# A router's hand-over between two expert paths: 48 instead of 32 tokens leave the feature matmuls, and 32 instead of 16 gathered rows come during the sums

## What is computed

```
q = (xt @ w_q).reshape(T, PEER_HEADS, 2, half)
s1, s2 = q0 . keys1, q1 . keys2              # 128 scores each, per head
v1, i1 = lax.top_k(s1, 16);  v2, i2 = lax.top_k(s2, 16)
sc, pos = lax.top_k(v1 + v2 (all 256 pairs), 16);  gate = softmax(sc)
u = jnp.take(u_tab, eb, axis=0)              # 128 rows of 1024 per token
a = jnp.einsum('nhkd,nd->nhk', u, xb)
w = jax.nn.gelu(a) * gb
vv = jnp.take(v_tab, eb, axis=0)
y = jnp.einsum('nhk,nhkd->nd', w, vv)
x = layer_norm(alpha * x + y)
```

## Time and profile before

| | |
|---|---|
| median of three runs | 1434.01 us (1432.75 to 1435.45) |
| the profiled execution | 1433.48 us, its span 1431.8 us |
| granted TensorE clock, mean over the span | 0.997 |
| busy in the span: PE, DVE, ACT, POOL | 1406.7, 1087.3, 606.7, 903.4 us |
| moved by DMA | 415.41 MB, mean 290 GB/s |

### The profile page before, as it was taken

How to read it: one execution, slowest core, us unless ns; L and a number is a source line. 1 busy time by engine, 2 the same in 40 slices (tenths; PEclk the granted TensorE clock), 3 DMA queues, 4 the chain that set the end, 5 groups by cost and what they waited for, 6 DMA issues and landing times.

```text
span 1431.8 us, 24761 instructions
## 1 busy us (share of the span) xinstructions
PE 1406.7 (98%) x8045; PEld 1248.2 (87%) x8045; DVE 1087.3 (76%) x2324; ACT 606.7 (42%) x1019; POOL 903.4 (63%) x595
## 2 busy tenths in 40 slices
PE   9999999999999999999999999999999999999996
PEld 5888878888999999999999999878888888888885
DVE  5366666688999998858774885987777777777786
ACT  5666751324333354454544443333333333333332
POOL 3422331335599978979888786766666666666744
PEclk9999999999999999999999999999999999999998
DMA  6213120423689979999999899999999999999981
GB/s 243 75 50 113 59 90 1 147 84 102 197 316 342 323 259 395 417 389 418 418 417 399 341 381 407 383 388 387 371 374 374 372 366 360 367 368 366 372 315 59
DMA packets 138959, 415.41 MB, mean 290 GB/s; under 512 B 13904, under 2 KB 56656, under 8 KB 136720
## 3 DMA queue, kind: packets, MB, share of 16 engines
q1 hardware_dynamic: 80128, 240.69, 45.9%
q0 software_dynamic: 42064, 151.15, 26.8%
q10 hardware_dynamic: 16704, 22.81, 4.3%
HBM read 363.89 MB, written 50.14 MB: 289 GB/s over the span
## 4 chain that ended last, share of the span: by engine, by line
PE 76%; DVE 8%; DMA 5%; POOL 4%; issue 3%; ACT 2%; SPq 1%; DVEq 0%; ACTq 0%; POOLq 0%
PE banks L2019 12%; PE banks L2021 11%; PE banks L2020 11%; PE banks L1964 11%; PE banks L1965 11%; PE banks L1966 11%; DMA raw<-v_tab 3%; POOL lo L501 2%; PE banks L2081 2%; PE banks L2237 1%; PE banks L2238 1%; POOL rows L822 1%; PE banks L2174 1%; DMA rows<-u_rows,expert_at 1%; DVE rows L1454 1%
## 5 line engine op out<-in xcount | busy, mean ns | idle before, releaser
L501 POOL TENSOR_TENSOR lo<-raw,hi 128x1024 fp32r<-128x1024 f32 x224 | 540.2, 2413 | 416.5 <-ACT hi L495 396.5
L1964 PE MATMUL banks<-x1T_hi,hi 128*128 128x352 f32 (+3 forms) x1168 | 389.9, 334 | 1.3 <-ACT kept L1106 1.0
L1965 PE MATMUL banks<-x1T_lo,hi 128*128 128x352 f32 (+3 forms) x1168 | 384.6, 329 | 0.0
L1966 PE MATMUL banks<-x1T_hi,lo 128*128 128x352 f32 (+3 forms) x1168 | 383.6, 328 | 0.0
L495 ACT ACTIVATE hi<-raw 128x1024 fp32r<-128x1024 f32 x291 | 305.6, 1050 | 57.0 <-DMA raw<-u_t 37.4
L2019 PE MATMUL banks<-hi,wgt_hi 128*128 128x512 f32 x750 | 292.1, 389 | 2.0 <-DVE wgt_lo L1811 1.9
L2020 PE MATMUL banks<-lo,wgt_hi 128*128 128x512 f32 x750 | 291.8, 389 | 0.0
L2021 PE MATMUL banks<-hi,wgt_lo 128*128 128x512 f32 x750 | 291.8, 389 | 0.0
L1964 PEld LDWEIGHTS banks<-x1T_hi,hi 128*128 128x128 f32 x1168 | 219.8, 188 | 6.2 <-ACT kept L1106 1.3
L1966 PEld LDWEIGHTS banks<-x1T_hi,lo 128*128 128x128 f32 x1168 | 220.3, 189 | 4.4
L1965 PEld LDWEIGHTS banks<-x1T_lo,hi 128*128 128x128 f32 x1168 | 220.1, 188 | 3.9
(11 more groups left out here) (245 smaller groups left out, 1846.7 us busy)
## 6 DMA issues: line engine op xcount, KB each, us to landing
raw<-u_t SPq DMA_DIRECT2D x128, 512.0 KB
raw<-v_tab SPq DMA_DIRECT2D x128, 512.0 KB
g_scratch<-stage SPq DMA_DIRECT2D x12, 2048.0 KB
gelu_scratch<-gelu ACTq DMA_DIRECT2D x116, 192.0 KB
ga<-gelu_scratch SPq DMA_DIRECT2D x29, 768.0 KB
gg<-g_scratch SPq DMA_DIRECT2D x14, 1536.0 KB
raw<-w SPq DMA_DIRECT2D x26, 512.0 KB
raw<-w_pq SPq DMA_DIRECT2D x16, 512.0 KB
```

The lines of the kernel that those rows point to most:

```text
L501: eng.tensor_tensor(l[:, :], raw[:, c % RAW_SLOTS, :], h[:, :].bitcast(F32), ALU.subtract).then_inc(odd_lo_ready if by_vector(c) else lo_r ...
L1964: pe.matmul(o, h[:, s], hiT[:, k, tokens], start=(k == 0), stop=False)
L1965: pe.matmul(o, h[:, s], loT[:, k, tokens], start=False, stop=False)
L1966: ins = pe.matmul(o, l[:, s], hiT[:, k, tokens], start=False, stop=(k == KT - 1))
```

## The change

Two sets of late tokens instead of one: 32 tokens with four lanes each as before, and 16 more with eight lanes each (16 ranks, so 16 more gathers in the feature stage). The feature matmuls go from 352 to 336 columns. `EXTRA` goes from 16 to 32, so the feature stage keeps 144 gathers and the sum stage has 16 more, with a third buffer `extra2` that lies where the gelu buffers were; octets 2 to 5 take three extra rows each, the others two. Their GELU and weights are made in two batches of 16. The second set needs another change of `x1_home` (`second_home`), and 8 more small moves each for x, numbers, gates and weights. The last six (instead of four) groups of tokens are `late_hots`. `turn_chosen` moves from the first tile of the first `two_chunks` to the second.

```diff
-LATE_TOKENS = 32
-SPREAD = P // LATE_TOKENS
+LATE_SETS = (32, 16)
+LATE_TOKENS = sum(LATE_SETS)
 LATE_AT = P - LATE_TOKENS
-LATE_RANKS = RANKS // SPREAD
+LATE_RANKS = sum(RANKS // (P // n) for n in LATE_SETS)
+LATE_MOVES = sum(P // n for n in LATE_SETS)
 FEATURED = DENSE - LATE_TOKENS
-EXTRA = 16
+EXTRA = 32
+EXTRA_BATCHES = (16, 16)
...
+CHOSEN_AT = 1
+FIRST_BATCH_AT = 8
...
+            if n < len(late_slots):
+                used_by = n // 2 - (HOT_SLOTS if n // 2 >= WHOLE_GROUPS else 0)
...
-        EXTRA_ASKED_AT, EXTRA_DOT_AT = (2, 4), (5, 7)
+        ASKED_AT = {2: (2, 4), 3: (0, 2, 4)}
+        DOT_AT = {2: (4, 6), 3: (2, 4, 6)}
...
+        def late_sets():
+
+            first, column = P, 0
+            for n in LATE_SETS:
+                first -= n
+                for g in range(P // n):
+                    yield slice(first, first + n), slice(n * g, n * (g + 1)), slice(column, column + n)
+                column += n
...
             def move_numbers():
 
                 sp.wait_ge(late_numbers_ready, 1)
-                for g in range(SPREAD):
-                    sp.dma_start(late_numbers[late_group(g), :],
-                                 block_numbers[LATE_AT:, late_group(g)]).then_inc(late_numbers_moved, 16)
+                for tokens, lanes, columns in late_sets():
+                    sp.dma_start(late_numbers[lanes, columns], block_numbers[tokens, lanes]).then_inc(late_numbers_moved, 16)
...
+            def move_second_x():
+
+                sp.wait_ge(selT_ready, 2)
+                for g in range(P // LATE_SETS[1]):
+                    sp.dma_start(late_x_second[LATE_SETS[1] * g:LATE_SETS[1] * (g + 1), :],
+                                 x1[LATE_AT:LATE_AT + LATE_SETS[1], TB - 1, :]).then_inc(late_x_moved, 16)
...
+                    if first and t == MID_TILES - 2:
+                        move_second_x()
...
-                            pool.wait_ge(late_numbers_moved, 16 * SPREAD)
+                            pool.wait_ge(late_numbers_moved, 16 * LATE_MOVES)
...
+            v_octet(0, 0, 2)
+            v_octet(0, 1, 2)
+
+            for slot in range(GELU_SLOTS):
+                pool.wait_ge(gelu_stored[slot], 16 * (A_PRE + A_MID) // GELU_SLOTS)
+            with pool.Fori(1, 3) as i:
+                v_octet(i, 0, 3)
+                v_octet(i, 1, 3)
+            with pool.Fori(3, OCTETS // 2 - 1) as i:
+                v_octet(i, 0, 2)
+                v_octet(i, 1, 2)
...
+            def second_home():
+
+                act.wait_ge(late_x_moved, 16 * LATE_MOVES)
+                act.wait_ge(row_used, R_PRE * ROWS + LATE_SETS[0])
+                home(late_x_second)
...
-                        if first and tile == 0:
+                        if first and tile == CHOSEN_AT:
                             take_turned()
...
-            two_chunks(0, first=True)
+            two_chunks(0, homes=3, first=True)
             two_chunks(1)
-            two_chunks(2, second=True)
+            two_chunks(2, homes=4)
+            two_chunks(3, homes=5)
```

More of the change, by code:

```diff
@@ L1161, in late_dots_done, with two_chunks @@
                 act.activation(late_gelu, late_dots, ACT.Gelu).then_inc(late_gelu_ready, 1)
-            def two_chunks(o, first=False, second=False, last=False):
+            def two_chunks(o, first=False, second=False, third=False, last=False):
                 for half in range(2):
@@ L1176, in two_chunks @@
                         if second and tile == 0:
+                            second_home()
+                        if third and tile == 0:
                             late_dots_done()
@@ L1187, in _ @@
             two_chunks(2, second=True)
-            with act.Fori(3, O_MID - 1) as o:
+            two_chunks(3, third=True)
+            with act.Fori(4, O_MID - 1) as o:
                 two_chunks(o)
@@ L1213, in _, with extra_gelu @@
                     split_hi(act, S_V + EXPERT_SLOTS + k, 2 * i)
+            def extra_gelu(batch):
+                ranks = slice(FIRST_EXTRA + sum(EXTRA_BATCHES[:batch]), FIRST_EXTRA + sum(EXTRA_BATCHES[:batch + 1]))
+                act.wait_ge(extra_kept, sum(EXTRA_BATCHES[:batch + 1]))
+                act.activation(dots_gelu[:, ranks], dots[:, ranks], ACT.Gelu).then_inc(dots_gelu_ready, 1)
+            with act.Fori(0, FIRST_BATCH_AT - 1) as i:
+                octet_hi(i)
+            extra_gelu(0)
+            with act.Fori(FIRST_BATCH_AT - 1, LAST_OCTET - 1) as i:
+                octet_hi(i)
             for i in (LAST_OCTET - 1, LAST_OCTET):
@@ L1750, in _, with two_chunks @@
             one_hots(0, 0, True)
-            def two_chunks(o, first=False, second=False, last=False):
+            def two_chunks(o, homes=None, first=False, last=False):
                 for tile in range(8):
@@ L1758, in two_chunks @@
                         one_hots(tile + 1, o, first and tile + 1 < HOT_SLOTS)
-                    if first and tile == 0:
-                        dve.wait_ge(homes_ready, 3)
-                    if second and tile == 0:
-                        dve.wait_ge(homes_ready, 4)
+                    if homes is not None and tile == 0:
+                        dve.wait_ge(homes_ready, homes)
                     for n in (2 * tile, 2 * tile + 1):
```

128 lines of the change are left out of this document (69 added, 59 removed).

## The result

The changed kernel takes 1466.9 us (median of four runs, 1466.0 to 1469.0) against 1433.7 in the same session: a ratio of 1.0232 (95% interval 1.0215 to 1.0250). The prediction was 1437.3 with a range of 1427 to 1444; the time lies 23 us outside it.

A forecast was written before the change was run, and what follows sets the result against it. PE, busy 98%, was taken to be held by DVE's routing, POOL's `lo` and DVE's late groups, losing its saving. 1433.5 + 3.3 by the start of the sums + 0.5 in them = 1437.3 us, range 1427 to 1444.

The forecast's parts named there:

- What PE saves: Feature matmuls: 16 fewer columns save 6.6 ns each, 0.16 us a tile, 20.5 us over 128 tiles.
- Tiles 0 to 46 lost: Before the first scatter: PE, 7.5 us earlier, waits for DVE's routing and one-hots and keeps only 0.9 us.
- The numbers' moves: SP's queue: twelve small moves instead of four start POOL 5.1 us later, holding PE to tile 57; costs 5.7 us (0 to 6.5).
- Other moves: First `two_chunks`: 16 more moves on SP's queue delay the load behind them; PE has two GELUs of slack; 1.5 us (0 to 4).
- The late groups: End of features: DVE is the chain; two more groups with third products cost 3.2 us each, 6.4 together (1.2 to 8).
- The sums: Sum stage: extra dots and gathers fit in DVE's idle time and the queues; 0.5 us for octets 2 to 5 (0 to 8).
- Rival E: Sum stage: DMA queues bind, with 383 GB/s as ceiling; total 1446 us, or 1442 if partly hidden; chance 0.17.
- three signs of being wrong: POOL's wait not longer by 4 us or more; added late groups costing 3 us together; PE idling in octets 2 to 5.

The follow-up runs named there:

- e4: e2 with the extra dots one tile later, at tiles 5 and 7 (3, 5, 7 in octets 2 to 5); 1455.0 us, ratio 1.0142.
- e5: e4 with POOL first waiting only for the first set's four number moves, and for the second set's eight where first used; 1448.2 us.
- e6: e5 with the second set's numbers behind the load of tile 48, its rows and all gates in the second `two_chunks`; 1454.1 us.
- e10: e9 with the two added late groups made as normal groups, the outer products of 16 tokens left out; 1446.4 us.
- e7: e4 with the two added late groups made as normal groups, the outer products of 16 tokens left out; 1449.3 us, ratio 1.0112.
- the seven kernels: The changed kernel and six follow-ups with its order of work in the features, e2, e4, e8 and e16 among them; sums begin at +10.2 to +13.2 us.
- e9: e5 with the second set's moves and the gates one or two ahead of each load over 24 tiles; 1448.7 us, ratio 1.0091.
- e11: e9 with only the third extra dot of octets 2 to 5 taken over 128 of 1024 columns; 1446.4 us.
- e15: e9 with the extra rows asked at tiles 0 and 2; 1453.6 us.
- e12: The kernel before with eight more small moves behind the four number moves, and POOL waiting for all twelve; 1439.6 us, ratio 1.0039.
- e2: The changed kernel with `late_gates` moved out of `small`, so that all tensors lie where they lay before; 1475.3 us, ratio 1.0292.
- e16: e2 with the extra rows asked at tiles 0 and 2 in octets 6 to 13 alone; 1453.4 us, ratio 1.0136.
- e8: e4 with all extra dots taken over 128 of 1024 columns, all gathers and waits kept; 1446.2 us, ratio 1.0084.
- e1: The kernel before with only `small` 32 floats wider, so tensors allocated after it lie 128 bytes later; 1446.3 us, ratio 1.0085.

## Why the prediction was wrong, step by step

- **What PE saves: right.** From tile 69 to 96 the changed kernel gains 4.1 us in 27 tiles, 0.15 a tile (0.16 predicted). But no more than that tile by tile; it was lost wherever something else was late.
- **Tiles 0 to 46 lost: right.** PE is 3.0 us early at tile 45, not 7.2, since POOL's `lo` holds it from tile 13 on already. That changes nothing, as the routing would have taken it.
- **The numbers' moves, 5.7: right in size, and shown.** POOL starts 6.4 us later (5.1 predicted); the split wait takes 5.8 us of the growth away against e4, some 5 against the others with e4's order, and the moves alone cost the kernel before 3.9 at tile 63 and 5.5 in the end.
- **Other moves, 1.5 (0 to 4): too small.** e5 to e6 shows 4.4 us more of the growth to tile 63, and 6.7 when the batches come later. The prediction set them against a slack of two GELUs; but the scatter's copy stands behind the waiting `hi` on ACT's list, and PE had no such slack for that (3.33 us at 606.04). Of the growth from tile 45 to 63 e6 still has 5.3; some of it is PE running into POOL, which was to be expected, and how much the eight moves at 565 us add wasn't separated.
- **The late groups, 6.4: right in kind, twice too large.** Left out, they give 2.9 and 3.0 by the start of the sums (e10, e7, against the means). One reason is in the rows: "nothing between" 0.6 and 3.0 us a product doesn't hold, the twelve of before already have 0.84, 0.99, 1.47 and 1.98. And the step's assumption that DVE decides there, whatever PE's lead, didn't hold in full: with the starts at +6.8 to +8.9 at tile 103 in the seven kernels, the sums began at +10.2 to +13.2, and with +2.5 to +5.0 in e9, e11 and e15 at +6.8 to +8.1.
- **The clock: a term that no step had.** The prediction's prices of matmuls are those of a granted clock of 1.00, and in the changed kernel it is 0.50, beside PE's waits, for 20.5 us of the feature stage: up to 10 us. The shift of +10.8 at the start of the sums, 7.5 more than predicted, holds that; e12, with one part of the change and the clock at 1.00, paid 3.9.
- **The sums, 0.5 (0 to 8): this is the step that failed, by 21.7 us**, with two faults of its own and the placement (next point). First, it looked for room in octets 2 to 5 and took octets 6 to 13 as free. It priced the wait by a row of before where the extra row is asked at tile 4 and used at 7 of its octet, and carried that landing time of at most 11.3 us over; but the diff puts the dots of octets 6 to 13 two tiles behind the request. In octet 8, say, the row is asked at 1181.70, DVE is free for it at 1191.04 and starts at 1193.50. That is worth 11.4 to 12.8 us once the matmuls are fast (the traces of e2 against those of e4 and e16). Second, DVE's room was taken as a mean over an octet (10.3 us idle), where what counts is the time between one `wgt_hi` and PE's need of `wgt_lo`, and each delay there can meet POOL's `lo`: 7.5 us in octets 0 to 6, 5.3 of them DVE's (e8).
- **What no step had: the placement.** The diff's `small` from P to P + 32 was read as space, and its cost taken as nothing. Alone it is worth 12 us (e1), 10 to 12 of them in the sums; taken away while the extra rows still land too late, nothing by e2's trace.
- **Rival E (the queues bind): wrong as a mechanism, though its side was right.** From 1114 to 1390 us e4 moves 386 GB/s at a share of 1.00 with PE busy 276.00 of 276 us, and in octets 2 to 5 e8, with all its gathers and short dots, moves 400 with PE busy 131.01 of 132 (before: 130.91):

```profile
1114.00:1390.00 276.00, 276.00 (x1220) 228.63 (x1219) 229.97 (x292) 100.26 (x137) 192.07 (x144) 1.00 1.00 386
```

```profile
972.00:1104.00 132.00, 131.01 (x577) 107.85 (x576) 115.52 (x150) 47.72 (x65) 93.74 (x77) 1.00 1.01 400
```

- **Its own signs.** Of the three signs of being wrong that the prediction names, two came: the added late groups cost some 3 us together, and PE idles 2.3 us for `wgt_lo` in octets 2 to 5 (1.1 before). POOL's wait is longer by 9.0 us, so that one didn't.

The sum as measured: +10.8 at the start of the sums in place of +3.3, 4 to 11 (7.5 in e4) for DVE in the first octets in place of 0.5, and 12 to 15 for the pair of placement and extra rows that land too late; 1433.7 + 33. Open stay how the +10.8 divides between moves, clock and late groups, and what makes four of e2's six executions 10 to 14 us slower than the other two.

## What to carry to other kernels

Read a diff for what it does to addresses as well as to work: when a tensor early in a stack grows, check where the matmul operands behind it land, and keep them where they were (here a multiple of 512 bytes). Price a wait by the time between request and use in the new code, not by a wait that the old code didn't have. When a repair of a shown cause gives nothing, look for a second limit of the same size before dropping the cause: here two repairs were worth 0 and 0 alone, and 12 us together. Look at the granted clock beside each new wait of PE: here the waits cost more than their length. And compare one trace with several of the same order of work before a difference of 2 or 3 us is given a cause.

## What was not expected of the hardware

- fp32r matmuls of 512 columns whose stationary operand starts 128 bytes past a multiple of 512 come 0.2325 us apart in place of 0.2266 (2.6%), at a granted clock of 1.00; the load instructions' own median stays at 188 ns in both. Only an offset of 128 bytes was tried, and not why it is so.
- SP's queue takes about as long for a small move of 16 rows as for one of 32, whether a row has 64 or 128 bytes or 4 KB: 2.57 us for four (0.64 each), 8.11 for twelve (0.68), 5.37 for the eight of x (0.67); other batches show 0.62 to 1.06, and spread out, most single ones 0.51.
- The granted clock falls to 0.50 for 3.4 or 6.8 us beside waits of PE of 1.3 to 3.7 us; matmuls of 336 columns then come 0.280 us apart in place of 0.153, those of 512 columns 0.43 in place of 0.227 (e15).
- A gather of 128 rows of 4 KB lands 9.5 to 10.5 us after its issue in the changed kernel's sum stage (6.1 to 11.1 in e16). The Trainium skill ("DMA: Bandwidth & Descriptors", "Anatomy of one DMA — SWDGE (gpsimd) path") fits 2.0 us and the bytes at 436 GB/s, an estimate of 3.2 us for 0.52 MB; under this load the trace shows three times that.
